# A two-block transformer kernel on one core: tokens become the stationary operand of every streamed product

## What is computed

```python
# first block
proj = rmsnorm(x, attn_norm_g) @ w_in                 # 2048 x 9216
u, v_sgu, q, k, v_att, g_a, g_b = split(proj)
y_a = spatial_gating(gelu(u), rmsnorm(gelu(v_sgu), sgu_norm_g), w_s, b_s)
y_b = stick_breaking_attention(rmsnorm(q), rmsnorm(k), v_att)      # 8 heads
merged = sigmoid(g_a) * (y_a @ w_up_a) + sigmoid(g_b) * (y_b @ w_up_b)
x = x + merged @ w_o
gate, up = split(rmsnorm(x, ffn_norm_g) @ w_ffn_in)    # 2048 x 11264
x = x + (silu(gate) * up) @ w_ffn_out                  # 5632 x 2048
x = x + sigmoid(rmsnorm(x, ple_norm_g) @ w_ple_gate) * (p @ w_ple)
# second block
z = rmsnorm(x, g_mix) @ w_in_2                         # 2048 x 3584: conv, pool and query parts
k, v = split(rmsnorm(mem, g_mem) @ w_kv)
mix = concat(conv_out, pool_out, cross_attention)      # 4 heads over 256 memories
x = x + mix @ w_out
u = causal_dwconv(rmsnorm(x, g_ffn) @ w_up, width 3)   # 2048 x 11264
x = x + (silu(gate) * val) @ w_down                    # 5632 x 2048
return rmsnorm(x, g_final)
```

## Time and profile before

| | us |
|---|---|
| median of 3 runs | 2572.57 (2572.35 to 2572.8) |
| the profiled execution, device time | 2572.37 |
| its span in the trace | 2570.6 |
| PE busy | 2550.7, 99% |
| PE weight loads busy | 2452.1, 95% |
| DVE busy | 1527.5, 59% |
| ACT busy | 1205.2, 47% |
| DMA | 471.41 MB, 183 GB/s over the span |

### The profile page before, as it was taken

The page is one execution under the profiler, slowest core; times in us unless marked ns, Lnnn a source line. Parts: engine busy times, 40 slices in busy tenths (PEclk is TensorE's granted clock), DMA queues, the critical chain, the costliest instruction groups (busy, mean ns, idle before and its releaser), DMA issues.

```text
span 2570.6 us, 43399 instructions
## 1 busy us (share of the span) xinstructions
PE 2550.7 (99%) x19064; PEld 2452.1 (95%) x19064; DVE 1527.5 (59%) x1815; ACT 1205.2 (47%) x1378; POOL 16.9 (1%) x18
## 2 busy tenths in 40 slices
PE   9999999999999999999999999999999999999997
PEld 7998999999999999998889999999999999998887
DVE  6565555665555555554555776775666666665454
ACT  6455555444444434444444554434545445444443
POOL 0000000000000000000000000010000000000000
PEclk9999999999999999999999999999999999999999
DMA  7655555556655655565666556466565655666663
GB/s 271 188 167 180 166 163 176 183 176 186 184 185 182 184 185 182 182 187 186 193 193 222 178 187 184 156 188 183 180 187 182 185 182 181 186 184 193 187 191 102
DMA packets 130222, 471.41 MB, mean 183 GB/s; under 512 B 14576, under 2 KB 14960, under 8 KB 129904
## 3 DMA queue, kind: packets, MB, share of 16 engines
q1 hardware_dynamic: 130032, 468.63, 58.3%
HBM read 466.47 MB, written 2.10 MB: 182 GB/s over the span
## 4 chain that ended last, share of the span: by engine, by line
PE 99%; ACT 0%; DVE 0%; DMA 0%; issue 0%; DVEq 0%; SPq 0%; ACTq 0%
PE ps L1288 92%; PE ps L1291 5%; PE ps L608 0%; PE ps L378 0%; PE ps L722 0%; ACT wh L1309 0%; DMA raw<-in_w_in 0%; PE ps L693 0%; PE ps L738 0%; PE ps L566 0%; DVE O L1228 0%; PE ps L968 0%; PE ps L932 0%; PE ps L278 0%; DVE wl L1310 0%
## 5 line engine op out<-in xcount | busy, mean ns | idle before, releaser
L1310 DVE TENSOR_TENSOR wl<-raw,wh 128x1024 fp32r<-128x1024 f32 x878 | 1074.4, 1226 | 1020.5 <-ACT wh L1309 1019.5
L1309 ACT CAST wh<-raw 128x1024 fp32r<-128x1024 f32 x878 | 917.6, 1046 | 1237.4 <-PE ps L1291 1232.4
L1288 PE MATMUL ps<-x4g_hi,wh 128*128 128x256 f32 x1408 | 399.2, 283 | 0.0
L1288 PE MATMUL ps<-x1g_hi,wh 128*128 128x256 f32 x1408 | 399.2, 283 | 0.0
L1288 PE MATMUL ps<-x1g_lo,wh 128*128 128x256 f32 x1408 | 399.0, 283 | 0.0
L1288 PE MATMUL ps<-x4g_lo,wh 128*128 128x256 f32 x1408 | 399.0, 283 | 0.0
L1288 PE MATMUL ps<-x4g_hi,wl 128*128 128x256 f32 x1232 | 349.1, 283 | 0.0
L1288 PE MATMUL ps<-x1g_hi,wl 128*128 128x256 f32 x1232 | 349.1, 283 | 0.0
L1288 PEld LDWEIGHTS ps<-x4g_hi,wh 128*128 128x128 f32 x1408 | 270.6, 192 | 0.0
L1288 PEld LDWEIGHTS ps<-x1g_hi,wh 128*128 128x128 f32 x1408 | 270.6, 192 | 0.0
L1288 PEld LDWEIGHTS ps<-x1g_lo,wh 128*128 128x128 f32 x1408 | 270.6, 192 | 0.0
(11 more groups left out here) (300 smaller groups left out, 4521.8 us busy)
## 6 DMA issues: line engine op xcount, KB each, us to landing
raw<-in_w_in SPq DMA_DIRECT2D x200, 512.0 KB, 3.7
raw<-in_w_ffn_in SPq DMA_DIRECT2D x176, 512.0 KB, 3.6
raw<-in_w_up SPq DMA_DIRECT2D x176, 512.0 KB, 4.2
raw<-in_w_ffn_out SPq DMA_DIRECT2D x88, 512.0 KB, 4.2
raw<-in_w_down SPq DMA_DIRECT2D x88, 512.0 KB, 3.6
raw<-in_w_o SPq DMA_DIRECT2D x32, 512.0 KB, 3.6
raw<-in_w_ple_gate SPq DMA_DIRECT2D x32, 512.0 KB, 3.9
raw<-in_w_out SPq DMA_DIRECT2D x32, 512.0 KB, 3.8
```

Of the source, the lines that this page charges most:

```text
L1288: pe.plain(lambda e, a=(dst, lhs, rhs), s=start, p=stop: e.matmul(*a, start=s, stop=p, skip_group_check=True))
L1309: hi = act.do(lambda e, r=r, slot=slot: e.copy(wh[:, r, :], raw[:, slot, :]), in_tok[s], free)
L1310: lo_tok[s] = dve.do(lambda e, r=r, slot=slot: e.tensor_tensor(wl[:, r, :], raw[:, slot, :], wh[:, r, :].bitcast(F32), ALU.subtract), hi)
```

## The change

All chunks except the two pool granules become form "N". `X` becomes `[128 tokens, 2, 2048]`, is loaded a second time in that layout (`load_rows`, four loads of 512 KB beside granules 100 to 130; the first product uses the old layout as `XT`), and the output leaves in that layout.

With tokens on partitions, the norms are sums along a row: `squares` uses ACT's accumulating Square, `rows_root` and `rows_invert` work on two numbers for each partition, `RT`. The products with ones for the norms of x are gone, except the small ones of the first norm and of the memory's norm; those for the heads' norms in `after_qk` are gone too. The scale by RT rides on the instruction that drains the chunk, most often on ACT.

What the next product needs with features on partitions is turned by PE, in groups of eight transposes for a chunk: 2 chunks of u, 4 of q and k, 4 of merged, 4 for x after each of w_o, w_ffn_out, w_ple and w_out, 7 of w_in_2 and 1 of the keys of the memory, 22 of w_up. For each of the 22 chunks of w_ffn_in, gate and up are multiplied before the turn, and four transposes do. w_down needs none (it had three groups of eight before; w_ffn_out had four). ACT or DVE then reads the turned tiles from PSUM banks 4 to 7.

The cross attention moves its third product from bank 6 to bank 4, since the turns of w_in_2 use banks 6 and 7. `after_pool` now also marks the pool chunk's banks free. The conv tiles move two steps later. At the end, the gain of the last norm is loaded as a broadcast 1 MB tile `GF`, and three quarters of x are multiplied by it before the last sum is known.

The diff, cut to its core:

```diff
-        def norm_sum(p_tok, norm):
...
+        def squares(n, tok, norm):
+            for b in range(2):
+                norm["sq"] = act.do(lambda e, b=b: e.activation(TB[:, 512 * b:512 * b + 512],
+                                                                X[:, b, 512 * n:512 * n + 512], ACT.Square,
+                                                                accum_out=SUMS[:, b, n:n + 1]),
+                                    tok, part_tok.get("tb"))
...
+        def stage_rows(chunk, dst, scale, *tokens):
+            tok = [act.do(lambda e, b=b: e.activation(dst[:, b, :], banks(chunk)[b], ACT.Copy, scale=scale[:, b:b + 1]),
+                          chunk.done, *tokens) for b in range(2)]
...
+        def unfold(s, n, tok, gname, dest, free, norm):
+            bk = 6 if norm is norm4 else 4 + 2 * (n % 2)
...
+            def b():
+                g["t"] = turn(X[:, :, 512 * n:512 * n + 512], tok, bk, 4)
+                for i in range(4):
+                    c = 4 * n + i
+                    hi = act.do(lambda e, c=c, i=i: e.activation(dest.hi[:, c, :], turned(bk, i), ACT.Copy,
+                                                                 scale=gain(gname, c)), g["t"], free())
...
+            at(s + 1, a)
+            at(s + 2, b)
...
         def after_ffn1(n):
...
+                def z():
+                    g["s"] = [act.do(lambda e, b=b: e.activation(ST[:, b, 0:T], banks(chunk)[b][:, 0:T], ACT.Silu,
+                                                                 scale=RT[:, b:b + 1]),
...
+                def a():
+                    g["t"] = st_tok["free"] = turn(ST, g["m"], bk, 2)
...
         for n in range(22):
-            last_ffn = gemm_chunk(t["w_ffn_in"], "T", x1g, pairs16, after_ffn1(n), n)
+            last_ffn = gemm_chunk(t["w_ffn_in"], "N", x1g, pairs16, after_ffn1(n), n)
...
-        def after_z(name, dst, i0):
+        def after_z(name, dst, i0, scale, norm, late):
             def after(s, chunk):
-                at(s + (3 if name == 0 else 1), lambda: z_tok.update({name: drain_rows(chunk, dst[:, i0:i0 + 4, :],
-                                                                                      norm4)}))
+                g = {}
+
+                def a():
+                    g["st"] = stage_rows(chunk, rows2, scale, norm["tok"], rows2_tok.get("free"))
+
+                def b():
+                    done = rows2_tok["free"] = turn(rows2, g["st"], 6, 4)
+                    z_tok[name] = [act.do(lambda e, i=i: e.copy(
+                        dst[:, i0 + 2 * i:i0 + 2 * i + 2, :].rearrange("p k t -> p (k t)"), ps[:, 6 + i, :]), done)
+                        for i in range(2)]
+                    bank_free[6], bank_free[7] = z_tok[name]
+                at(s + late, a)
+                at(s + late + 2, b)
...
-                conv_tile(ch.last + RING + 2 + i, j)
+                conv_tile(ch.last + RING + 4 + i, j)
...
                 chunk.drained = [mix.ready[6 + 3 * q + 2]]
+                bank_free[chunk.bank] = bank_free[chunk.bank + 1] = chunk.drained
             return after
```

More of the change, by code:

```diff
@@ L276, in norm_sum @@
         def norm_sum(p_tok, norm):
-            norm["sum"] = pe.do(lambda e: e.matmul(ps[:, 7, 0:T], ones, part[:], start=True, stop=True), p_tok)
-            if norm.get("rt") is not None:
-                for b in range(2):
-                    norm["sum"] = pe.do(lambda e, b=b: e.matmul(ps[:, 6, b:b + 1], part[:, b * P:(b + 1) * P],
-                                                                ones[:, 0:1], start=True, stop=True))
+            for b in range(2):
+                norm["sum"] = pe.do(lambda e, b=b: e.matmul(ps[:, 6, b:b + 1], part[:, b * P:(b + 1) * P],
+                                                            ones[:, 0:1], start=True, stop=True), p_tok, bank_free[6])
@@ L794, in after_ub @@
+                at(s + 2, a)
             return after
@@ L880, in a @@
                     bank_free[4] = bank_free[5] = tok
[L881 to L886 removed]
+                    xs = X[:, :, 512 * n:512 * n + 512]
@@ L887, in after_ple @@
+                    xt = st_tok["free"] = dve.do(lambda e: e.tensor_tensor(xs, xs, ST, ALU.add), tok)
+                    unfold(s + late, n, xt, "mix", x3g, lambda: out1.done, norm4)
+                late = 2 if n == 0 else 1
+                at(s + late, a)
             return after
         for n in range(4):
-            last_pg = gemm_chunk(t["w_ple_gate"], "T", x2g, pairs16, after_pgate(n), n)
-            gemm_chunk(t["w_ple"], "T", pp, (0,), after_ple(n), n, 4)
+            last_pg = gemm_chunk(t["w_ple_gate"], "N", x2g, pairs16, after_pgate(n), n)
@@ L1151, in two_block_kernel, with load_gf @@
         fin = {}
[L1153 to L1164 removed]
+        def load_gf():
+            fin["gf"] = loads.load(s_gf, GF[:], t["gfin"].partition_broadcast(P), last_up.done)
@@ L1166, in after_down, with store @@
+        at(len(granules) + RING, load_gf)
+        def store(b, c0, c1, tok):
+            fin["out"] = loads.load(s_out, out[:, b, c0:c1], X[:, b, c0:c1], tok)
         def after_down(n):
             def after(s, chunk):
-                tok = []
-                turns = chunk.kind == "N"
-                g = {}
-                def turned():
-                    g["t"] = st_tok["free"] = turn(g["st"], 4, 4)
-                def add():
-                    for b in range(2):
-                        xs = X[:, 4 * n + 2 * b:4 * n + 2 * b + 2, :].rearrange("p k t -> p (k t)")
-                        src = turned_banks(4)[b] if turns else banks(chunk)[b]
-                        tok.append(dve.do(lambda e, src=src, xs=xs: e.tensor_tensor(xs, src, xs, ALU.add),
-                                          g["t"] if turns else chunk.done))
-                    if turns:
-                        bank_free[4], bank_free[5] = tok
-                    else:
-                        chunk.drained = list(tok)
@@ L1200, in b @@
-                def b():
-                    part_tok["tb"] = fold(TB, n == 0, g["sq"])
-                def c():
-                    norm6["sum"] = pe.do(lambda e: e.matmul(ps[:, 7, 0:T], ones, part[:], start=True, stop=False),
-                                         part_tok["tb"])
-                def d():
-                    fin[n] = [act.do(lambda e, c=c: e.activation(X[:, c, :], X[:, c, :], ACT.Copy,
-                                                                 scale=gain("fin", c)), g.get("sq"), fin.get("sq"))
-                              for c in range(4 * n, 4 * n + 4)]
@@ L1211, in after, with a, b @@
-                at(s + 1, a)
-                at(s + 4, d)
-                if n == 3:
-                    norm_end(s + 2, norm6)
-                else:
+                sl = slice(512 * n, 512 * n + 512)
+                tok = [dve.do(lambda e, b=b: e.tensor_tensor(X[:, b, sl], banks(chunk)[b], X[:, b, sl], ALU.add),
+                              chunk.done) for b in range(2)]
+                chunk.drained = list(tok)
+                if n < 3:
+                    def a():
+                        squares(n, tok, norm6)
+                    def b():
+                        fin[n] = dve.do(lambda e: e.tensor_tensor(
+                            X[:, :, sl], X[:, :, sl], GF[:, sl].unsqueeze(1).broadcast_to([P, 2, 512]), ALU.mult),
+                            norm6["sq"], fin["gf"])
+                    at(s + 1, a)
@@ L1219, in after_down @@
+                sp.wait([fin["out"]])
             return after
         for n in range(4):
[L1222 to L1233 removed]
@@ L1301, in two_block_kernel @@
         beside = {6: lambda: load_x(6), 7: lambda: load_x(7), 8: load_constants, 16: load_sgu}
+        for q in range(4):
+            beside[100 + 10 * q] = lambda q=q: load_rows(q)
         steps = max(max(todo) + 1, total + RING)
```

447 lines of the change are left out of this document (206 added, 241 removed).

## The result

The changed kernel took **2526.93 us** (median of 4 runs, 2523.7 to 2528.49), beside 2572.48 for the kernel before on the same chip (4 runs, 2572.35 to 2572.8): a ratio of 0.9821, 95% interval 0.9804 to 0.9838. It is faster by 1.8%. The prediction said 2518 and a range of 2505 to 2532. The profiled execution is the fastest of the runs, 2523.7, with a span of 2521.9; it is compared with the before's profiled execution (2572.4, span 2570.6).

The account below looks back on a forecast made before the run. PE, busy 99% of the span, was taken as the bound. From the profiled 2572.4: form -109.1, turns +53.5, products with ones -9.9, tail -4.3, waits +15.3 give 2517.9, forecast 2518 us, range 2505 to 2532.

Parts of the forecast that it names:

- Part 1, the form: 682 granules go from 24 to 12 matmuls each, 2.880 to 2.720 us: 109.1 us less.
- Rival 3: Columns alone decide: granules stay near 2.85 us in form N, the form saves 22, time 2605; chance 1%.
- Part 2, the turns: PE's transposes: 56 turns of eight at 0.89, 22 of four at 0.45, less 6.2 already there: 53.5 us more.
- Rival 2: Each transpose costs its whole 273 ns on PE's path: 78 us more, 2596, slower than before; chance 2%.
- Part 3, products with ones: Head norms and seven row norms of 256 columns leave PE: 9.9 us less.
- Part 4, the tail: From the last granule's last matmul to the span's end, 16.9 us become 12.5: 4.3 less, bounds 2 to 6.
- Part 5, the waits: New PE waits for ACT or DVE, with the clock behind them: 15.3 us more, bounds 9 to 24.
- The pool turn: Last turn of w_in_2 waits for DVE to drain the second pool granule's bank: 6.7 us, bounds 5 and 8.
- The scores: Cross attention, third product now in bank 4: scores and third product wait, 3.0 us, between 0 and 6.
- The clock: PE's clock may fall after the 6.7 us pool wait: 2.3 us to get back, bounds 0 and 4.
- Rival 1, turns that wait: A late source at each of the 78 turns stops PE, 0.3 us each: 2541; chance 6%.
- Rival 4: Waits at the pool turn and conv tiles are absent, only the head waits stay: 2506; chance 6%.

Follow-up runs that it names:

- e8_gate: e5_warm24 with the sigmoid of the fourth gate chunk issued one step later, behind the exponential of that step: 2505.39 us, ratio 0.9736.
- e6: e5_warm24 with w_ffn_in back in the form with stationary weights, without its turns of four and its per-token scale: 2525.06 us, ratio 0.9812.
- e7: e5_warm24 with w_up back in the form with stationary weights, without its turns of eight and its per-token scale: 2515.23 us, ratio 0.9774.
- e5_warm24: e3_conv3 with 24 warm-up matmuls in place of 16: 2507.01 us, ratio 0.9742.
- e1_own6: The changed kernel with the turn of the last chunk of w_in_2 put into that chunk's own two PSUM banks: 2518.04 us, ratio 0.9788.
- e3_conv3: e2_own_all with each conv tile one step earlier: 2508.57 us, ratio 0.9749.
- e2_own_all: e1_own6 with all turns of w_in_2 and the memory's keys in their chunks' own banks, cross attention's third product back in bank 6: 2513.53 us, ratio 0.9766.
- e4_fill: The changed kernel with 24 matmuls of unused result added ahead of the turn of the last chunk of w_in_2: 2524.05 us, ratio 0.9809.
- e9_swap: e8_gate with the two destination bank pairs of the turned tiles of w_up swapped: 2505.55 us, one run.

## Why the prediction was right, and where it was off

**What bounds the kernel: right.** Every difference of the experiments could be read off as PE's own time or PE's wait. In e8_gate, with these waits taken away, PE's waits behind the first granules come to 2.1 us in 2480, 1.6 of them for `mats`, as before the change.

**Part 1, the form: right to a tenth.** 2.880 became 2.720 in all stages, and two of them were turned back alone (e6, e7) with 0.160 a granule both times. The rule that was weighed there, the section "Back-to-back issue gap" of the Trainium skill's page "TensorE: Matmul & The Clock Gate", is given for isolated matmuls and would have had N's and T's granules 0.03 apart; e6 and e7 speak against it for this stream, which loads new weights for each matmul. By that section's figures the form would be worth 682 x 0.030 = 20.5 us, an estimate, where the prediction has 22. Whether the matmul or its load is what costs the excess, no run here tells apart. Rival 3 falls.

**Part 2, the turns: right in kind, 1.8 too small.** A turn of eight costs 0.91 in the mean, not 0.89, 56 times (0.9 in all); one of four 0.48 in the changed kernel, not 0.45, 22 times (0.7). The value for four was read from the chain as the length of the piece, and the switch back to long matmuls was undersized. By the prediction's own sign (a turn of w_up over 0.89) this term was wrong, by 2%. Rival 2, the transpose at its whole 273 ns, falls: e7 would have come out 20 below e5_warm24 and not 8.2 above.

**Part 3, products with ones: right,** 9.8 for 9.9. **Part 4, the tail:** 5.2 instead of 4.3, within the bounds given. The chain has its seven small instructions at about 0.2 each, as the estimate said; the first store is issued at 2514.84, 4.7 behind the start of the last granule's last matmul, for "some 5", and from there to the end of the span are 7.1, for 7.2. Both parts were right to 0.3. The rest of the difference is in the sum itself: its terms, 5, 5.2 and 2, make 12.2 and not 12.5, and the old tail, counted the same way, was 17.0 and not 16.9.

**Part 5, the waits: the mechanisms were right, the sum was 3.7 too small.** Its bounds, 9 to 24, are not quite what the bounds of its terms add up to, 8.3 to 21.3; 19.0 lies within both.
- The pool turn: 6.63 for 6.7, shown by e1_own6, which took just this wait away.
- The conv tile: 2.9 for 2.9, shown by e3_conv3; with the gap behind it its granule is 3.1 longer.
- The scores: 3.9 and 0.6 in gaps for 3.0, within the bounds, shown by e2_own_all. The choice to halve the before's lateness because ACT had taken over drains was the weak part of this term.
- The clock: 3.1 for 2.3. One piece was priced at 2.3, behind the pool turn, and it cost 1.5. The wait of 2.9 at the scores drew a second one, of 1.6, which no term had. Both the price, 0.8 too high, and the count were off, and in part made up for each other: the same cost had to be asked of every wait, also of the shorter ones. That the sum of the clock came out near is partly luck, since the pieces come and go between executions.
- after_qk and the like: 0.8 for 0.4 (granule 45 and the turn that waits for L880).
- What was missing: 0.9 at L747. The granule behind that wait is 1.4 longer; against it stand 0.5 that a short wait at head 1 cost before and that are gone. Behind the 1.4 is the order of sigmoid and exponential on ACT, with a table load each. The prediction went through distances in steps and through DVE's queue, but not through the order of ACT's functions. e8_gate shows it.

**What no term had:** 1.2 for small products. The same groups of two to eight products cost mostly 0.02 to 0.05 more each where they stand between N granules: L747's pair and its neighbour 0.680 where 0.647 stood before, the group of L731 and L702 1.380 for 1.333, four products of L939 0.913 for 0.860.

**Rival 1, turns that wait,** did not come: of 78 turns one shows a wait for its source, the 0.3 for L880. (The wait of the pool turn is for its bank.) **Rival 4** did not come: both waits were there. Its 2506, for a kernel without the waits at the pool turn and the conv tiles, is close to the 2505.4 of e8_gate, but that is luck: e8_gate also lacks the waits of the heads, the one at L747 and the lower clock at the start. With all its waits left out the prediction's own sum would have been 2502.6.

**The median.** The sum was made for the profiled execution, and there it missed by 5.8 (2523.7 to 2517.9). The other 3.2 up to the median are a step the prediction did not have: it took the 0.2 between profile and median of the kernel before for that of the changed one. The profiled execution was also the fastest of the four, so comparing with it flatters the prediction; by the medians the gain was 45.6 for 54.5. A kernel that has idle pieces on PE has a spread of its own, and e5_warm24, with its pieces closed, has 0.33.

## What to carry to other kernels

Take PE's price of a form or of a group from the distance of starts in the stream it is to stand in, and count the matmuls with their loads, not the columns alone; go through the order of functions on ACT as well as on DVE, with a table load where the function changes; then list each bank and each tile whose last reader now stands in the same step as its next writer on PE, since such waits can be read off in advance: two of three came out to a tenth, the third 0.9 short. Ask of each such wait what the clock behind it costs, also at 2 to 3 us, and expect the spread of the times to grow with them. A turn that goes into the bank pair that its own chunk has just left needs nobody else's drain.

## What the runs showed of the chip that was not expected

- TensorE's clock after an idle piece isn't the same in each execution. Behind the same 2.9 us wait at the conv tile it was 1.00 in the changed kernel's profile (11 matmuls in 2.76) and 0.50 in that of e1_own6 (4.36); behind the 2.9 us wait at the scores it was 0.50 in the changed kernel's and 1.00 in those of e1_own6 and e4_fill; behind the gap at the start of the launch it was 1.00 in the kernel before (2.2 us) and 0.50 in e1_own6 (2.1). With the gaps closed or short, four runs lay within 0.33 us (e5_warm24) and within 0.31 (e8_gate).
- Eight transposes of 128 columns with 273 ns each in the records cost 0.89 to 0.93 together between matmuls of 512 columns, four cost 0.47 to 0.49; which of the two values comes changes from turn to turn and isn't set by the destination banks (e9_swap).
- Two functions of ACT with different tables in one step cost 1.28 for each load. With a sigmoid and two such loads ahead of it, an exponential that PE waits for came some 4 us later, and that was worth 1.4 of the whole time.
